# One upper-half copy of a weight tile moved between the two odd/even exponentials of the attention steps

## The chip, the cores and the metric

The kernel runs on one core of a Trainium2 chip. The metric is device time in microseconds (us) of one execution. The engines are named as in the profile: PE (TensorE, matmuls), PEld (its weight loads), DVE (VectorE), ACT (ScalarE), POOL (GpSimd) and SP (SyncE, which here only issues DMAs). Each engine carries out its own instructions in the order in which the program lists them, and engines wait for one another on semaphores.

## The reference, cut to what matters

A sequence of 256 tokens of width 1024 goes through a first block (a gated mixer, a neighbourhood attention and 64 experts) and then through a second block of two equal layers. The change touches only the attention part of these two layers:

```python
proj = x @ w_in            # q_sb k_sb v_sb q_mb k_mb v_mb g_sb g_mb
z = einsum(q_sb, k_sb) * scale                       # stick-breaking attention
log_keep = where(past, log_sigmoid(-z), 0)
suffix = cumsum(log_keep, reverse=True) - log_keep
w = where(past, exp(log_sigmoid(z) + suffix), 0)
o_sb = w @ v_sb
o_mb = moba_attention(rope(q_mb), rope(k_mb), v_mb)  # with 256 tokens a causal softmax attention
merged = sigmoid(g_sb) * (o_sb @ w_branch_sb) + sigmoid(g_mb) * (o_mb @ w_branch_moba)
x = layer_norm(alpha * x + merged @ w_out); x = layer_norm(alpha * x + swiglu(x))
```

## The kernel before

Large fp32 matmuls are made out of three passes over operands split in two: an upper half (the value rounded to fp32r) and a lower half (what is left). For every weight tile of 128 x 2048 values that lands in `weight_ring`, ACT writes the upper half (`high`, a Copy of the whole tile, line 1822) and DVE then subtracts it for the lower half (`low`, line 2494). PE waits for the lower half (`wait_split`) before it uses the tile. The upper halves have a few places (`high_place`), so `high` first waits until the weights have landed and until the job that last read its place is done (`wait_used`).

A layer's attention has six steps, p = 0 to 5: three of the stick-breaking attention (`p < NS`, NS = 3) and three of the other one. In each step PE runs, in this order: `scores(p)` (line 1438), `weighted_sum(p - 1)` (line 1464), the step's "fillers" (`FILLERS_OF_STEP`: parts of x @ w_in that do not depend on the attention, 24 matmuls of 512 columns each, line 957), and `weights_turn(p)` (eight transposes, line 908). Each filler output of 512 columns has two weight tiles, one for each half of the contraction, and two token tiles t = 0, 1. `NEXT_CHUNK[p]` names the two weight tiles of the next filler output, whose halves are made in step p: "vm" in step 0, "gs" 0 in step 1, "gs" 1 in step 2, then "gm" 0, "gm" 1 and "bs".

In a stick-breaking step the scores of the even heads (side 0) and of the odd heads (side 1) are in two banks. ACT takes the absolute value of both, Exp of both, Ln of both. DVE then makes the logarithm of the weights, first for side 0 and then for side 1 (`stick_b`, lines 2649 to 2663; each ends with an increment of `log_weights`). ACT takes Exp of side 0 and of side 1 as each is ready (line 1927), then makes the two upper halves of `NEXT_CHUNK[p]`, then moves out the remaining fillers (`gate_out`, line 1860), and then copies the transposed weights from their banks to `wT_` (`weights_out`, line 1870), for which the next step's `weighted_sum` waits. In step 2 ACT's order behind the filler of that step is thus: Exp side 0, Exp side 1, high, high, gate_out(7), weights_out(2). PE's order at that place is filler 7, weights_turn(2), scores(3), weighted_sum(2), filler 8.

The order of all this is written out by hand in the program. `NEXT_CHUNK`, the tiles' places in the rings and the semaphore counts follow from one list (`SPLIT_UNITS`), in whose order both ACT and DVE go through the tiles.

Of the kernel before, what the change touches and what calls it, by code (L numbers as in the profile page):

```python
# [156 lines left out]
NS = len(STEPS)  # L157
# [7 lines left out]
def plan():  # L165
# [188 lines left out]
    for r in (main, long, hold, units):  # L354
# [17 lines left out]
NEXT_CHUNK = {p: [("l_in", *name, half) for half in range(2)]  # L372
              for p, name in ((0, ("vm", 0)), (1, ("gs", 0)), (2, ("gs", 1)), (3, ("gm", 0)), (4, ("gm", 1)))}
# [24 lines left out]
def high_place(key, layer):  # L398

    if layer and key in FIRST_UNITS:  # L400
        return 4 + FIRST_UNITS.index(key)
    return HIGH_PLACE[SPLIT_UNITS.index(key)]
# [16 lines left out]
def build(nc, a):  # L419
    banks, units, freed_by, sources, order, last_jobs = plan()  # L420
    ctx = ExitStack()
    with ctx:
# [5 lines left out]
        def sem(name):  # L428
            if name not in sems:
                sems[name] = ctx.enter_context(nc.semaphore(name))  # L430
            return sems[name]
# [163 lines left out]
        def bank(key):  # L595
            return psum[banks[key][0]]
# [7 lines left out]
        def wait_full(eng, key, it=0):  # L604

            b, n, per = banks[key]
            eng.wait_ge(bank_full[b], n + 1 + it * per)
# [9 lines left out]
        def out(ins, key):  # L617
            ins.then_inc(bank_free[banks[key][0]], 1)
# [8 lines left out]
        def wait_weights(eng, key, it=0):  # L627
            s, n, per = units.place[key]
            eng.wait_ge(landed[s], 16 * (n + 1 + it * per))
# [11 lines left out]
        def upper(key, it):  # L641
            if key in FIRST_SPLIT:
                at = FIRST_UPPER[FIRST_SPLIT.index(key)]
                return ring_low[:, at, :] if at < SLOTS else first_upper[:, at - 10240:at - 10240 + SLOT]
            place = high_place(key, it)
            return high_ring[:, place, :] if place < 4 else high_late[:, (1, 2, 0)[place - 4], :]
# [7 lines left out]
        def wait_used(eng, key, it):  # L654
            job = freed_by[key]
            if job[0] == "down":
                eng.wait_ge(sem("down_done"), (FT // 2 - 1) * (it + 1) + job[1] + 1)
            else:
                wait_full(eng, job, it)
# [185 lines left out]
        def _(pool):  # L845
# [3 lines left out]
            for i, (col, n, _) in enumerate(pieces[:2]):  # L849
                pool.dma_start(bias[:, i, 0:n], bcast("b_in", col, n)).then_inc(sem(f"bias_landed{i}"), 16)  # L850
# [764 lines left out]
        def _(act):  # L1615
# [197 lines left out]
            def high(layer, *key):  # L1813

                u = SPLIT_UNITS.index(key)
                wait_weights(act, key, layer)
                earlier = [(l, v) for l in range(layer + 1) for v in range(NU) if (l, v) < (layer, u)]
                for l, v in reversed(earlier):
                    if high_place(SPLIT_UNITS[v], l) == high_place(key, layer):
                        wait_used(act, SPLIT_UNITS[v], l)  # L1820
                        break
                A(upper(key, layer), ring[:, units.place[key][0], :], ACT.Copy).then_inc(sem("high_ready"), 1)  # L1822
# [21 lines left out]
            for layer in range(L2):  # L1844
# [11 lines left out]
                def gate_out(i):  # L1856
                    name, n, t = FILLERS[i]
                    if name in ("gs", "gm"):
                        wait_full(act, (name, n, t), layer)
                        out(A(gates[("gs", "gm").index(name)][:, t, n * CHUNK:(n + 1) * CHUNK], bank((name, n, t))[:, :],  # L1860
                              ACT.Copy), (name, n, t))

                def sums_out(t):
                    wait_full(act, ("sums", t), layer)
                    out(A(inverse[0:2, :], bank(("sums", t))[0:2, :], ACT.Copy), ("sums", t))

                def weights_out(p):
                    for side in range(2):
                        wait_full(act, ("wT", p, side), layer)
                        out(A(wT_[:, side, :], bank(("wT", p, side))[:, :], ACT.Copy), ("wT", p, side))  # L1870

                def values_out(p):
                    b, t = p // NS, STEPS[p % NS][0]
                    if p % NS in LAST_OF_TILE:
                        act.wait_ge(sem("values_summed"), 2 * TT * layer + TT * b + t + 1)
                        values = bank(("o", b, t))[:, :].rearrange("p (f q) -> p f q", q=P)
                        if b == 0:
                            if t == 0:

                                wait_used(act, ("l_in", "km", 0, 0), layer)  # L1880
                            A(oTs[:, 0, :, t * P:(t + 1) * P], values, ACT.Copy).then_inc(sem("o_left_high"), 1)
                        else:
                            if t:
                                act.wait_ge(sem("o_right"), TT * layer + t)
                            out(A(o32, values, ACT.Copy), ("o", b, t))

                def values_high(t):
                    act.wait_ge(sem("o_scaled"), TT * layer + t + 1)
                    A(oTm[:, 0, :, t * P:(t + 1) * P], o32, ACT.Copy).then_inc(sem("o_right_high"), 1)

                for p in range(2 * NS):
                    t, fs = STEPS[p % NS]
                    keys = P * (t + 1)
                    if p < NS:
                        at = 2 * NS * layer + 2 * p
                        for side in range(2):
                            wait_full(act, ("sc", p, side), layer)
                            A(es[:, side, :], bank(("sc", p, side))[:, :], ACT.Abs).then_inc(sem("abs_ready"), 1)
                        for side in range(2):
                            act.wait_ge(sem("abs_ready"), at + side + 1)  # L1900
                            A(es[:, side, :], es[:, side, :], ACT.Exp, scale=-1.0).then_inc(sem("exp_done"), 1)
                        for side in range(2):
                            act.wait_ge(sem("exp_done"), at + side + 1)
                            A(es[:, side, :], es[:, side, :], ACT.Ln, bias=1.0).then_inc(sem("ln_done"), 1)
                    else:
                        for side in range(2):
                            act.wait_ge(sem("mb_max"), 2 * NS * layer + 2 * (p - NS) + side + 1)
                            for j, f in enumerate(fs):
                                hh = t * H2 + 2 * f + side
                                last = A(rw[:, side, j * keys:(j + 1) * keys], bank(("sc", p, side))[:, j * keys:(j + 1) * keys],  # L1910
                                         ACT.Exp, bias=mbn[:, hh:hh + 1], accum_out=mbs[:, hh:hh + 1])
                            out(last, ("sc", p, side))
                    if p:
                        values_out(p - 1)
                    gate_out(FILLERS_OF_STEP[p][0])
                    if p == NS - 1:
                        for name, dst in (("qmT", q2), ("kmT", k2)):
                            for t in range(TT):
                                wait_full(act, (name, t), layer)
                                A(dst[:, 0, :, t * P:(t + 1) * P], bank((name, t))[:, :].rearrange("p (f q) -> p f q", q=P),  # L1920
                                  ACT.Copy).then_inc(sem("heads_high"), 1)
                    if p == 2 * NS - 1:
                        values_high(0)
                    if p < NS:
                        for side in range(2):
                            act.wait_ge(sem("log_weights"), at + side + 1)
                            A(rw[:, side, :], rw[:, side, :], ACT.Exp).then_inc(sem("stick_weights"), 1)
                    if p == NS + 1:
                        sums_out(0)
                    if p in NEXT_CHUNK:  # L1930
                        for half in range(2):
                            high(layer, *NEXT_CHUNK[p][half])
                    for i in FILLERS_OF_STEP[p][1:]:
                        gate_out(i)
                    weights_out(p)
# [929 lines left out]
```

## Time and profile before

| | |
|---|---|
| median of 3 runs | 1672.85 us (1669.48 to 1673.49) |
| the profiled execution's own time | 1673.72 us |
| its span, first to last instruction | 1671.9 us |
| PE busy | 1612.7 us, 96% of the span |
| DVE / ACT busy | 842.9 us (50%) / 596.6 us (36%) |
| mean granted TensorE clock | 0.987 |
| attention steps of layer 0 / layer 1 in the trace | about 927 to 1036 us / 1316 to 1425 us |

The profile has a page of the whole span and views of the trace behind it: the waits of one engine, the instructions in order of time, and busy time with granted clock in given stretches. PE is busy nearly all the time, so a change on ACT can only matter where PE stands still or runs at its lower clock because of ACT. In a timeline row, "[2.65 <-ACT ...]" is the idle time of the engine just before this instruction and the engine that ended it. Durations of merged rows are from the first start to the last end; neighbouring rows of one engine can overlap a little, since instructions are pipelined.

### The profile page before, as it was taken

The page shows a single profiled execution, that of the slowest core. Times are in us where ns is not written, and L with a number is a line of the kernel's source. Part 1 is how long each engine was busy: PE and PEld are TensorE (multiplying, and loading weights), DVE is VectorE, ACT ScalarE, POOL GpSimd, SP SyncE. Part 2 cuts the span into 40 slices and gives each one's busy share as a digit, 9 for nine tenths or more (in the row PEclk, how much of TensorE's full clock was granted, in tenths as well). Part 3 has the DMA queues.
Part 4 walks back from the last instruction along what each step waited for, and adds up shares of the span by engine and source line. Part 5 has one row for each costly group of instructions (what it writes and reads, how often), then busy time and mean ns, then how long its engine had stood idle before and what let it go on. Part 6 is the DMA issues. An engine that isn't in the chain of part 4 may idle for free.

```text
span 1671.9 us, 21860 instructions
## 1 busy us (share of the span) xinstructions
PE 1612.7 (96%) x9158; PEld 1144.0 (68%) x9159; DVE 842.9 (50%) x1186; ACT 596.6 (36%) x815; POOL 27.7 (2%) x48
## 2 busy tenths in 40 slices
PE   5999999999999999999999999999999999999998
PEld 2975545874444444444447877799998877799997
DVE  3639825753222222222227765865447684865454
ACT  2504432321111111111124666444343565644432
POOL 0200010000000000000000000000000000000000
PEclk8999999999999999999999999999999999999999
DMA  9956874556999999999984435456445542555540
GB/s 357 235 198 239 308 274 176 196 201 258 421 421 421 420 421 421 421 421 421 421 323 145 153 116 198 144 187 213 166 153 200 177 150 103 201 178 200 165 163 25
DMA packets 148434, 418.55 MB, mean 250 GB/s; under 512 B 6977, under 2 KB 55249, under 8 KB 123313
## 3 DMA queue, kind: packets, MB, share of 16 engines
q1 hardware_dynamic: 126048, 271.19, 44.8%
q10 hardware_dynamic: 17568, 127.93, 18.4%
q0 software_dynamic: 4720, 18.03, 3.7%
q8 instruction: 74, 1.21, 0.3%
q14 instruction: 24, 0.19, 0.0%
HBM read 416.07 MB, written 2.95 MB: 251 GB/s over the span
## 4 chain that ended last, share of the span: by engine, by line
PE 90%; DVE 5%; ACT 2%; issue 1%; SPq 1%; DMA 1%; DVEq 0%; ACTq 0%
PE bank L957 20%; PE bank L1309 14%; PE bank L1603 12%; PE bank L1320 7%; PE bank L1553 6%; PE bank L1291 4%; PE bank L939 4%; PE bank L1330 4%; PE bank L972 3%; PE bank L908 3%; PE bank L1133 3%; PE bank L1574 3%; DVE ring_low L2494 1%; SPq L735 1%; DMA weight_ring<-in_w_ada 1%
## 5 line engine op out<-in xcount | busy, mean ns | idle before, releaser
L2494 DVE TENSOR_TENSOR ring_low<-weight_ring,high_ring 128x2048 fp32r<-128x2048 f32 x92 | 207.9, 2287 | 59.9 <-ACT high_ring L1822 59.5
L1309 PE MATMUL bank<-weight_ring,arena 128*64 128x512 f32 x800 | 232.1, 592 | 0.7 <-DVE arena L2414 0.7
L957 PE MATMUL bank<-high_ring,split 128*128 128x512 f32 x608 | 201.5, 406 | 0.2 <-DVE split L2501 0.2
L957 PE MATMUL bank<-ring_low,split 128*128 128x512 f32 x448 | 180.8, 404 | 0.0
L1309 PEld LDWEIGHTS bank<-weight_ring,arena 128*64 128x64 f32 x800 | 74.5, 137 | 150.2 <-issue 150.2
L1822 ACT ACTIVATE high_ring<-weight_ring 128x2048 fp32r<-128x2048 f32 x92 | 171.6, 1905 | 10.5 <-PE bank L957 5.9
L1603 PE MATMUL bank<-split,ring_low 128*128 128x256 f32 x576 | 162.6, 282 | 0.0
L1603 PE MATMUL bank<-split,high_ring 128*128 128x256 f32 x832 | 148.9, 281 | 0.0
L957 PEld LDWEIGHTS bank<-high_ring,split 128*128 128x128 f32 x608 | 117.7, 194 | 33.2 <-issue 3.4
L1603 PEld LDWEIGHTS bank<-split,high_ring 128*128 128x128 f32 x832 | 128.8, 189 | 0.7
L1320 PE MATMUL bank<-weight_ring,arena 128*64 128x512 f32 x400 | 120.5, 598 | 0.6 <-DVE arena L2414 0.6
L2473 DVE SCALAR_TENSOR_TENSOR arena<-bank,cols,arena 128x256 f32<-128x256 f32 x33 | 16.0, 484 | 193.0 <-ACT arena L1790 193.0
L1309 PE MATMUL bank<-arena 128*64 128x512 f32 x256 | 112.5, 592 | 0.0
L2488 DVE TENSOR_TENSOR split<-bank,split 128x512 fp32r<-128x512 f32 x66 | 45.6, 691 | 125.9 <-ACT split L1804 125.9
L1603 PEld LDWEIGHTS bank<-split,ring_low 128*128 128x128 f32 x576 | 108.8, 189 | 0.0
L957 PEld LDWEIGHTS bank<-ring_low,split 128*128 128x128 f32 x448 | 86.0, 192 | 17.8
L1804 ACT ACTIVATE split<-bank 128x512 fp32r<-128x512 f32 x66 | 39.4, 597 | 146.0 <-PE bank L1320 146.0
L1790 ACT ACTIVATE arena<-bank 128x256 f32<-128x256 f32 x33 | 12.7, 384 | 209.0 <-PE bank L1309 209.0
L1291 PEld LDWEIGHTS bank<-routed 128*128 128x128 f32 x544 | 66.7, 190 | 27.4 <-issue 27.4
L908 PE MATMUL bank<-const,arena 128*128 128x128 f32 (+1 forms) x530 | 75.9, 282 | 6.8 <-DVE arena L2755 3.0
L1320 PEld LDWEIGHTS bank<-weight_ring,arena 128*64 128x64 f32 x400 | 34.4, 136 | 68.6 <-issue 68.6
L2785 DVE TENSOR_TENSOR arena<-arena,bank 128x256 f32<-128x256 f32 x44 | 18.5, 420 | 122.0 <-ACT arena L1965 122.0
(327 smaller groups left out, 2796.5 us busy)
## 6 DMA issues: line engine op xcount, KB each, us to landing
weight_ring<-in_w_in SPq DMA_DIRECT2D x62, 1024.0 KB, 8.2
weight_ring<-in_w_e_gate SPq DMA_DIRECT2D x49, 1024.0 KB, 9.2
weight_ring<-in_w_e_up ACTq DMA_DIRECT2D x46, 1024.0 KB, 13.7
weight_ring<-in_w_e_down ACTq DMA_DIRECT2D x46, 1024.0 KB, 13.0
weight_ring<-in_w_ada SPq DMA_DIRECT2D x24, 1024.0 KB, 11.7
weight_ring<-in_w_ffn_gate SPq DMA_DIRECT2D x22, 1024.0 KB, 5.5
weight_ring<-in_w_ffn_up SPq DMA_DIRECT2D x22, 1024.0 KB, 8.1
weight_ring<-in_w_ffn_down SPq DMA_DIRECT2D x22, 1024.0 KB, 6.1
```

The costliest lines, as they stand in the source:

```text
L908: return nc.tensor.transpose(dst, src, k("ident")[0:m, 0:m])
L939: last = mm(bank(key)[:, 0:cols_], left[:, n, t * P:(t + 1) * P], wv[:, j, :], start=(n == 0), stop=(n == kts * len(units_) - 1))
L957: last = mm(bank(key)[:, :], left[a_][:, n, t * P:(t + 1) * P], wv[b_][:, j, :], start=(n == 0 and i == 0), stop=(n == kts * len(units_) - ...
L972: last = mm(bank(key)[:, s_ * S:(s_ + 1) * S], halves(uk, CHUNK, it)[a_][:, n % 4, f * P:(f + 1) * P], right[b_][:, n, :], start=(n == 0 a ...
L1291: last = mm(down_banks[j][:, s_ * QUAD * CAP:s_ * QUAD * CAP + n], h2s[:, part, t, kt, :], onehot[:, q % 2, t, 0:n], start=(t == 0 and par ...
L1309: last = mm(hidden_bank[side * CAP:(side + 1) * CAP, :].rearrange("p (j n) -> p j n", n=FF), xgT[:, p // 2 % 2, kt, at:at + CAP], hidden_u ...
L1320: last = mm(down_banks[n][side * CAP:(side + 1) * CAP, :], hidT[:, p % 2, at:at + CAP], down_unit(e % DOWN_UNITS)[:, f, n * CHUNK:(n + 1) ...
L1330: last = mm(y_bank(n, t)[:, :], sent[:, p % 3, t * P:(t + 1) * P], ys[:, part, n * CHUNK:(n + 1) * CHUNK], start=False, stop=(p == PAIRS a ...
L1553: last = mm(bank(key)[:, :], fh[:, (2 * d + f) % 4, a_, t * P:(t + 1) * P], wv[b_][:, f, n * CHUNK:(n + 1) * CHUNK], start=(d == 0 and f = ...
L1603: last = mm(bank(key)[:, j * S:(j + 1) * S], wv[a_][:, kt, f * P:(f + 1) * P], xs[:, b_, kt, :], start=(kt == 0 and i == 0), stop=(kt == K ...
L1822: A(upper(key, layer), ring[:, units.place[key][0], :], ACT.Copy).then_inc(sem("high_ready"), 1)
L2494: V.tensor_tensor(lower(key), ring[:, units.place[key][0], :], upper(key, layer), ALU.subtract)\
```

## The change

In steps 0, 1 and 2 of each layer the first of the two `high` copies of `NEXT_CHUNK[p]` is issued between Exp of side 0 and Exp of side 1; the second one stays where it was, behind Exp of side 1. Steps 3 to 5 keep both where they were. The order of the upper halves among themselves is the same, and nothing is added or left out. The diff:

```diff
@@ -1925,10 +1925,13 @@
                         for side in range(2):
                             act.wait_ge(sem("log_weights"), at + side + 1)
                             A(rw[:, side, :], rw[:, side, :], ACT.Exp).then_inc(sem("stick_weights"), 1)
+                            if side == 0:
+
+                                high(layer, *NEXT_CHUNK[p][0])
                     if p == NS + 1:
                         sums_out(0)
                     if p in NEXT_CHUNK:
-                        for half in range(2):
+                        for half in range(p < NS, 2):
                             high(layer, *NEXT_CHUNK[p][half])
                     for i in FILLERS_OF_STEP[p][1:]:
                         gate_out(i)
```

## Rows read from the trace of the kernel before

**Rows 1.** The page's chain of work that ended last, shares by engine.

```profile
PE 90%; DVE 5%; ACT 2%; issue 1%; SPq 1%; DMA 1%; DVEq 0%; ACTq 0%
```

**Rows 2.** PE's waits in 870 to 1130: us in total, times, longest us.

```profile
PE bank L1464 <- ACT arena L1870: 3.1, 2, 2.7
```

**Rows 3.** Timeline of ACT, layer 0, step 2: start us, us, instruction, [idle before].

```profile
980.00 0.63 ACT L1927 ACTIVATE arena<-arena 128x512 f32<-128x512 f32 x1
982.99 0.63 ACT L1927 ACTIVATE arena<-arena 128x512 f32<-128x512 f32 x1 [2.36 <-DVE arena L2663]
983.53 3.70 ACT L1822 ACTIVATE high_ring<-weight_ring 128x2048 fp32r<-128x2048 f32 x2
987.13 0.58 ACT L1860 ACTIVATE arena<-bank 128x512 f32<-128x512 f32 x1
987.61 1.07 ACT L1870 ACTIVATE arena<-bank 128x512 f32<-128x512 f32 x2
```

**Rows 4.** Timeline of PE, layer 0, ends of steps 0, 1 and 2.

```profile
948.96 1.09 PE L1464 MATMUL bank<-arena 128*64 128x128 f32 x16
...
966.77 1.03 PE L908 MATMUL bank<-const,arena 128*128 128x128 f32 x8
...
983.65 1.03 PE L908 MATMUL bank<-const,arena 128*128 128x128 f32 x8
...
988.83 1.09 PE L1464 MATMUL bank<-arena 128*64 128x128 f32 x16 [2.65 <-ACT arena L1870]
```

**Rows 5.** Timeline of DVE, layer 0, end of step 2.

```profile
982.53 0.42 DVE L2663 TENSOR_TENSOR arena<-arena,const 128x256 f32<-128x256 f32 x1
985.46 4.49 DVE L2494 TENSOR_TENSOR ring_low<-weight_ring,high_ring 128x2048 fp32r<-128x2048 f32 x2 [2.50 <-ACT high_ring L1822]
```

**Rows 6.** Timeline of PE, layer 1, the same place.

```profile
1377.34 1.98 PE L1464 MATMUL bank<-arena 128*64 128x128 f32 x16 [2.66 <-ACT arena L1870]
```

**Rows 7.** Stretches: us, busy PE PEld DVE ACT POOL, granted clock, DMA share, GB/s.

```profile
929.00:930.00 1.00, 1.00 (x4) 0.81 (x3) 1.00 (x1) 1.00 (x2) 0.00 (x0) 0.50 1.05 406
990.00:991.00 1.00, 1.00 (x4) 0.81 (x5) 0.97 (x2) 0.00 (x0) 0.00 (x0) 0.70 0.95 354
1376.00:1377.00 1.00, 0.00 (x0) 0.00 (x0) 1.00 (x2) 1.00 (x3) 0.00 (x0) 0.55 1.03 395
```

**Rows 8.** Timelines: weighted sum of step 3, and gate_out after the next filler tile.

```profile
997.27 0.60 ACT L1860 ACTIVATE arena<-bank 128x512 f32<-128x512 f32 x1 [2.23 <-PE bank L957]
...
1004.51 1.09 PE L1464 MATMUL bank<-arena 128*64 128x128 f32 x16
...
1011.39 0.60 ACT L1860 ACTIVATE arena<-bank 128x512 f32<-128x512 f32 x1 [2.62 <-PE bank L957]
...
1386.78 0.60 ACT L1860 ACTIVATE arena<-bank 128x512 f32<-128x512 f32 x1 [3.22 <-PE bank L957]
```

**Rows 9.** Timeline of PE, three other stops in layer 0.

```profile
927.14 1.56 PE L1438 MATMUL bank<-split 64*128 64x128 f32 x24 [1.67 <-issue]
...
977.39 0.66 PE L908 MATMUL bank<-const,arena 128*128 128x128 f32 x4 [0.56 <-DVE split L2710]
...
1061.87 1.10 PE L908 MATMUL bank<-const,arena 128*128 128x128 f32 x8 [1.51 <-DVE arena L2755]
```

**Rows 10.** Timeline of ACT, layer 0, steps 0 and 1.

```profile
943.60 0.63 ACT L1927 ACTIVATE arena<-arena 128x512 f32<-128x512 f32 x1 [3.55 <-DVE arena L2663]
...
950.02 1.15 ACT L1901 ACTIVATE arena<-arena 128x512 f32<-128x512 f32 x2
...
960.38 0.63 ACT L1927 ACTIVATE arena<-arena 128x512 f32<-128x512 f32 x1 [1.93 <-DVE arena L2663]
...
967.40 1.09 ACT L1870 ACTIVATE arena<-bank 128x512 f32<-128x512 f32 x2 [2.78 <-PE bank L908]
```

**Rows 11.** SP's load of gs 1, first tile; the page's median time to landing.

```profile
925.91 0.51 SPq L735 DMA_DIRECT2D weight_ring<-in_w_in  x1
...
weight_ring<-in_w_in SPq DMA_DIRECT2D x62, 1024.0 KB, 8.2
```

## Prediction

> **What bounds the kernel now.** I read the page's chain first: 90% of it is PE [rows 1]. ACT work that is moved is worth nothing unless PE stands still for it, so the next view is the list of PE's waits around the attention of layer 0. One line in it is ACT's to answer for: the weighted sum (line 1464) waited for `weights_out` (line 1870) twice, 3.1 us in all, of which one stop has 2.7 [rows 2]; layer 1 has the same line again with the same numbers. The timeline of PE puts the long one at the end of step 2: 2.65 us of idle time before 988.83 in layer 0 [rows 4] and 2.66 us before 1377.34 in layer 1 [rows 6]. The reader should see there that the stop begins at 988.83 - 2.65 = 986.18, where the scores of step 3 end, and that nothing but the two copies of line 1870 ends it.
>
> The timeline of ACT tells why these copies are late [rows 3]. Exp of side 0 ends at 980.63, ACT idles 2.36 us until DVE has the logarithms of side 1, and only then, in one unbroken row, come Exp side 1 (982.99), the two `high` copies (983.53 to 987.23), gate_out (987.13) and the two weights_out (987.61 to 988.68). PE starts 0.15 us later. From 982.99 on, ACT is the path and each microsecond of it is paid by PE, while 2.36 us of ACT just before were empty.
>
> A second cost hangs on the same stop: the clock. The granted clock is 0.70 in 990 to 991 and 0.55 in 1376 to 1377 [rows 7], which is a mixture of its two levels, 2.4 GHz (1.00) and 1.2 GHz (0.50). What a low clock does is read from equal work at either level. From the start of the weighted sum to the gate_out behind the first filler tile it is 1011.39 - 1004.51 = 6.88 us in step 4, at full clock, but 997.27 - 988.83 = 8.44 us behind the stop in layer 0 and 1386.78 - 1377.34 = 9.44 us in layer 1 [rows 4, 6, 8]. So the clock costs 1.56 us in layer 0 and 2.56 us in layer 1, 4.12 us together.
>
> **The change, part by part.**
>
> *Step 2, where PE waits.* A pair of `high` copies lasts 3.70 us, and from the first start to the gate_out behind them it is 987.13 - 983.53 = 3.60 us, so one copy takes 1.80 us of ACT's sequence and about 1.90 us from start to end [rows 3]. Placed behind Exp side 0 (which lets its successor begin some 0.1 us before its end, at 980.54 as 983.53 follows 982.99) it runs to 982.44. DVE's last operation for side 1 ends at 982.53 + 0.42 = 982.95 [rows 5], so Exp side 1 still starts at 982.99, with 0.5 us to spare. Behind it now stands one copy and not two: gate_out comes at 985.33, weights_out at 985.81 to 986.88, and PE's weighted sum 0.15 us later, at 987.03. The stop shrinks from 2.65 to 0.85 us. That is 1.80 us per layer, 3.60 us for both; layer 1 has the same intervals [rows 6]. gate_out itself does not become the later one: its filler ends where the transposes begin, at 983.65 [rows 4].
>
> *What could hold the moved copy.* It waits for its weights, for its place, and for nothing else. The first tile of gs 1 is issued by SP at 925.91, and the median load of this kind lands in 8.2 us, so near 934 [rows 11]. Its place was last read by the fillers of vm, which end where the transposes of step 1 start, at 966.77 [rows 4]. Both are more than 13 us before 980.5. SP itself waits for PE's banks, not for `high`, so no load moves because of the copy; POOL has no part in this.
>
> *Activation tables.* The copy now stands between two Exps. In step 0 the same Copy already runs behind the Exps, and the next Exp, at 950.02, follows copies and absolute values with no table load ahead of it [rows 10]. I count zero. Were there a reload after every copy, it would show as rows of their own; the trace has none.
>
> *DVE.* Its order is unchanged. The lower halves of gs 1 begin today at 985.46, 2.50 us of them idle time spent on ACT [rows 5]. With the upper half ready at 982.44, the first can begin at 982.95; the second waits for the second copy, which still starts at 983.53 and now ends at 985.43, and takes about 2.25 us, half of the pair's 4.49. So DVE is done near 987.7 and not at 989.95. PE's next filler, at 987.03 + 1.02 = 988.05, finds both, and DVE's share of step 3 begins 2.2 us sooner, more than PE's 1.80. What is next late for the weighted sum is still ACT (0.85 us: the second copy), not DVE.
>
> *Steps 0 and 1: costed at nothing.* ACT idles 3.55 us (step 0) and 1.93 us (step 1) before Exp side 1 [rows 10], so the copy of 1.80 to 1.90 us fits in both, in step 1 with hardly anything over. But nobody waits for what follows. In step 0 the weighted sum at 948.96 has no idle time before it [rows 4], and in step 1 weights_out waits 2.78 us for PE's transposes [rows 10]. The cover is PE's filler; if it were gone, step 1 would lose the 0.0 to 0.1 us by which the copy may outlast ACT's gap, and it would gain, not lose, up to the 1.80 us. Bounds for both steps: 0.1 us lost to 0.1 us gained for each layer; I take 0.
>
> *The clock.* The trace does not show a stop of 0.85 us at this place, so its cost is bounded from both sides: 0 (the clock stays up, all 4.12 us come back) to 4.12 us (it falls as now). The nearest rows: a stop of 0.56 us at 977.39 left the clock at 1.00, and even 1.51 us before 1061.87 did, with dense work around it; 1.67 us before 927.14, followed by short matmuls, brought it to 0.50 [rows 7, 9]. In layer 1 the clock fell when PE had been idle from 1374.68 to somewhat past 1376 (0.55 over 1376 to 1377), that is after over 1.3 us of idle time [rows 6, 7]. In layer 0 the first 0.8 us of the stop, with the same transposes and scores ahead of it, passed without a fall; the drop came in 990 to 991, after all 2.65 us. 0.85 is nearest to 0.56 and below each stop that cost anything, so I take 0 and keep the other end for the range.
> The Trainium skill, "TensorE: Matmul & The Clock Gate", section "What's actually happening", says that the low clock is the default, that activity releases it, and that the moment of judgement does not start with the kernel, so that runs of one kernel differ. The trace agrees: the same stop of 2.65 us brought the fall after its end in layer 0 and within it in layer 1. By that page a short stop can still fall in a bad moment, which is the second rival below.
>
> *Sum.* 3.60 us of shorter stops + 4.12 us of clock = 7.72 us. Against the profiled execution: 1673.72 - 7.7 = 1666.0. That execution lies 0.87 us above the median of 1672.85, against which the same gain gives 1665.1. I put the time at 1665.6, between them. Later work follows PE: the loads are released by PE's banks, and later stops, such as that of 1.51 us at 1061.87, are made of a chain that itself starts from PE's results, so I expect the whole gain to reach the end.
>
> **The rivals.**
>
> *A. Forecast: both stops shrink and the clock holds.* 1665.6 us, own range 1663 to 1667.5 (the runs before spread over 4 us). Chance 0.63.
>
> *B. The stops shrink but the clock falls all the same.* The stretch of transposes, short score matmuls, 0.85 us of idle time and the short weighted sum is still thin work. Both layers lose the clock: 1672.85 - 3.6 = 1669.2, or 1670.1 from the profiled execution; in one layer only, about 1667.6. For it: 1.67 us at 927.14 was enough there. Against: that is twice as long. Chance 0.13 for both layers, 0.12 for one.
>
> *C. The move gives nothing at the end.* Something behind step 2 takes the gain back: for example DVE's maxima of step 3 or the fillers' weights. It would be 1672 to 1673. Against it: no row of PE's waits between 988.83 and the end of step 3, and DVE gains more than PE. Chance 0.07. That the change does not do what it says would look the same; I see no way to it, as ACT's order is the program's.
>
> *D. Slower: the moved copy is held and blocks Exp side 1.* ACT runs in order, so Exp side 1, the transposes behind it (PE at 983.65) and weights_out queue behind the copy. If it starts X later than 980.54, Exp side 1 starts at 982.44 + X. The saving of 1.80 us and the spare 0.55 us are used up at X = 2.35, so from a release at 982.9 on the kernel is slower, by 2 us for every further microsecond (two layers); more than 5 us slower needs a release behind 985.4, giving 1678 or more. Against: load and place are ready near 934 and at 966.77. The remaining mishap is low-clock stretches at new places, some 1.6 to 2.6 us each. Chance 0.05.
>
> **How the numbers follow.** 0.3% of the time, 5.0 us, is about what a measurement of this kernel can tell from no change, so "faster" means below 1667.8. A counts as faster nearly whole (0.61 of 0.63), as does most of the one-layer case (0.08 of 0.12). B in both layers, C and the rest are within 0.3%: 0.26 with part of D. Slower: 0.03. Hence faster 0.70, same 0.27, slower 0.03. The range leaves out C and D at the top and ends with B at 1670.3; at the low end it allows for the spread of the runs, one of which lay 3.4 us below the median: 1662.5.
>
> **What the profile of the changed kernel would show.** In step 2 of each layer, a single `high` between the two Exps of line 1927, Exp side 1 still 2.99 us behind Exp side 0, and one `high` behind it; the wait of line 1464 for line 1870 at 0.8 to 0.9 us in place of 2.65; a granted clock of 1.00 over the filler that follows. If the stop is 0.85 and the clock 0.5 behind it, B is right. If Exp side 1 starts late, D is. If line 1464 starts 1.8 us earlier and some later wait is that much longer, C is. The prediction is wrong in its larger half (4.12 of 7.72 us) if the clock does not follow the stop's length.

## The result and the profile after

| | kernel before | changed kernel |
|---|---|---|
| median of 6 runs each, side by side on one chip | 1670.04 us (1667.20 to 1673.49) | 1662.22 us (1660.95 to 1664.54) |
| ratio, 95% interval | | 0.9948 (0.9938 to 0.9958) |
| profiled execution / its span | 1673.72 / 1671.9 us | 1662.30 / 1660.5 us |
| mean granted clock | 0.987 | 0.992 |

The kernel is faster by 0.52%: 0.0052 x 1670 = 8.7 us (7.0 to 10.4). The two medians themselves differ by 7.8 us, which lies in the same interval. The forecast was 7.7 us less than before and 1665.6 us, with a range from 1662.5 to 1670.3. The direction and the size of the gain came out; the time itself lies 0.28 us below the range.

The timeline of ACT, layer 0, end of step 2, of the changed kernel answers to [rows 3]: start us, us, instruction, [idle before].

```profile
976.03 0.63 ACT L1927 ACTIVATE arena<-arena 128x512 f32<-128x512 f32 x1
976.57 1.90 ACT L1822 ACTIVATE high_ring<-weight_ring 128x2048 fp32r<-128x2048 f32 x1
979.03 0.63 ACT L1927 ACTIVATE arena<-arena 128x512 f32<-128x512 f32 x1 [0.56 <-DVE arena L2666]
979.57 1.90 ACT L1822 ACTIVATE high_ring<-weight_ring 128x2048 fp32r<-128x2048 f32 x1
981.37 0.58 ACT L1860 ACTIVATE arena<-bank 128x512 f32<-128x512 f32 x1
981.84 1.07 ACT L1870 ACTIVATE arena<-bank 128x512 f32<-128x512 f32 x2
```

Exp side 1 starts 979.03 - 976.03 = 3.00 us behind Exp side 0, against 2.99 in [rows 3]: the moved copy delays nothing, with 0.56 us to spare. There is no table load between the copy and the Exp. The trace does have rows of table loads (ACT_TABLE_LOAD, 1.28 us each), one ahead of each pair of Lns and one ahead of Exp side 0, in both kernels; where the prediction says that the trace has none, it holds only for the places behind a copy that stands between Exps. From Exp side 1 to the first weights_out it is 2.81 us and was 4.62. The timelines of PE (layer 0 and layer 1) and of DVE answer to [rows 4, 6, 5]:

```profile
983.06 1.09 PE L1464 MATMUL bank<-arena 128*64 128x128 f32 x16 [0.82 <-ACT arena L1870]
...
1368.28 1.09 PE L1464 MATMUL bank<-arena 128*64 128x128 f32 x16 [0.83 <-ACT arena L1870]
```

```profile
978.57 0.42 DVE L2666 TENSOR_TENSOR arena<-arena,const 128x256 f32<-128x256 f32 x1
978.91 2.28 DVE L2497 TENSOR_TENSOR ring_low<-weight_ring,high_ring 128x2048 fp32r<-128x2048 f32 x1
981.50 2.29 DVE L2497 TENSOR_TENSOR ring_low<-weight_ring,high_ring 128x2048 fp32r<-128x2048 f32 x1 [0.30 <-ACT high_ring L1822]
```

The stop has shrunk from 2.65 to 0.82 us, and DVE makes the first lower half without waiting, as worked out. The stretches behind the stops, to be read with [rows 7] (us, busy PE PEld DVE ACT POOL, granted clock, DMA share, GB/s):

```profile
984.00:991.00 7.00, 7.00 (x34) 5.62 (x31) 3.41 (x7) 4.54 (x19) 0.00 (x0) 1.00 0.45 171
1369.00:1376.00 7.00, 7.00 (x37) 5.59 (x33) 3.63 (x8) 4.34 (x19) 0.00 (x0) 1.00 0.47 178
```

The clock is at its upper level, 2.4 GHz, in both layers. In layer 0, from the weighted sum to the next gate_out it is now 989.97 - 983.06 = 6.91 us, where it was 8.44:

```profile
989.97 0.60 ACT L1860 ACTIVATE arena<-bank 128x512 f32<-128x512 f32 x1 [1.08 <-PE bank L957]
```

The profiled spans differ by 11.4 us, which is more than the change did. Three steps of the chain in order of time divide it, first of the kernel before, then of the changed one: the keys' matmuls ahead of the attention of layer 0, and the first long group of the feed-forward part in each layer.

```profile
902.75 22.72 PE bank L972 x192
1092.71 14.39 PE bank L1574 x120
1482.11 14.39 PE bank L1574 x120
```

```profile
898.79 22.72 PE bank L972 x192
1085.51 14.39 PE bank L1574 x120
1470.67 14.39 PE bank L1574 x120
```

Up to the first the changed kernel is 3.96 us ahead, before anything of the change has run. From the first to the second it gains 189.96 - 186.72 = 3.24 us, from the second to the third 389.40 - 385.16 = 4.24 us, and behind that nothing (0.04 us). So the change itself is worth 7.5 us in this pair of profiles, and the other 4 us belong to the two executions. In the fourteen profiles at hand the keys' matmuls of layer 0 start between 898.79 and 902.75 us, and not by kernel: s2_only, which has the move in step 2 as well, starts them at 902.61. The kernel before has the latest start of all. The 4 us arise in the first 43 us, where PE waits for the first loads and the clock is low for some time (over 35 to 40 us it is 0.50 before and 0.76 after); in the chain or the timeline of PE it is this row, before and after:

```profile
42.64 13.43 PE bank L939 x64
```

```profile
38.75 13.41 PE bank L939 x64
```

### The profile page after: what moved, and what is told of

Its sections match the earlier page's. It is cut to its first block, busy times and chain, and to the rows that moved or that the text cites. A ratio compares the mean times of both kernels' runs of the same rounds, so it can differ in the third digit from the quotient of the medians.

```text
span 1660.5 us, 21860 instructions
## 1 busy us (share of the span) xinstructions
PE 1606.6 (97%) x9158; PEld 1139.0 (69%) x9159; DVE 842.8 (51%) x1186; ACT 597.2 (36%) x815; POOL 27.6 (2%) x48
## 4 chain that ended last, share of the span: by engine, by line
PE 90%; DVE 5%; ACT 1%; issue 1%; SPq 1%; DMA 1%; DVEq 0%
PE bank L957 20%; PE bank L1309 14%; PE bank L1603 12%; PE bank L1320 7%; PE bank L1553 6%; PE bank L1291 4%; PE bank L939 4%; PE bank L1330 4%; PE bank L972 3%; PE bank L908 3%; PE bank L1133 3%; PE bank L1574 3%; DVE ring_low L2497 1%; SPq L735 1%; DMA weight_ring<-in_w_ada 1%
## 5 line engine op out<-in xcount | busy, mean ns | idle before, releaser
L1822 ACT ACTIVATE high_ring<-weight_ring 128x2048 fp32r<-128x2048 f32 x92 | 172.3, 1906 | 10.4 <-PE bank L957 5.8
```

## The experiments

The runs were made in three groups, each compared with the kernel before on the same chip: 1671.92 us (median of 15 runs) for s2_only, s01_only, both_between and early; 1671.30 (21 runs) for fill_stop2, fill_stop0_before, fill_stop0_after and fill_stop0_early; 1670.81 (23 runs) for fill_stop2_short, fill_stop0_short_before, fill_stop0_short_early and pad512. A line behind an inserted one has a higher number in that run's rows: the weighted sum, 1464, can be L1465 or L1466, and weights_out, 1870, can be L1871 to L1873. Stops are in us, of the one profiled execution of each.

| run | ratio, 95% interval | stop of the weighted sum, end of step 0 (layer 0, 1) | end of step 2 | low clock behind step 2's stop |
|---|---|---|---|---|
| kernel before | 1 | 0, 0 | 2.65, 2.66 | both layers |
| changed kernel | 0.9948 (0.9938 to 0.9958) | 0, 0 | 0.82, 0.83 | none |
| s2_only | 0.9955 (0.9941 to 0.9969) | 0, 1.46 | 0.86, 0.86 | none |
| s01_only | 0.9986 (0.9976 to 0.9997) | 0, 0 | 2.67, 2.63 | layer 0 |
| both_between | 0.9942 (0.9929 to 0.9956) | 0, 0 | 0, 0 (0.56 at the transposes) | none |
| early | 0.9936 (0.9922 to 0.9949) | 0, 0 | 0, 0 | none |
| fill_stop2 | 1.0000 (0.9991 to 1.0009) | 0, 1.56 | filled, too long | none |
| fill_stop2_short | 0.9985 (0.9977 to 0.9994) | 0, 1.60 | filled, 0.70 and 0.71 left | none |
| fill_stop0_before | 1.0005 (0.9995 to 1.0014) | 0.62, 0.72 | 2.63, 2.66 | both |
| fill_stop0_after | 0.9945 (0.9932 to 0.9959) | 0, 0 | 0.86, 0.83 | none |
| fill_stop0_early | 0.9940 (0.9926 to 0.9953) | 0, 0 | 0, 0 | none |
| fill_stop0_short_before | 0.9994 (0.9985 to 1.0002) | 1.60, 1.59 | 2.66, 2.62 | both |
| fill_stop0_short_early | 0.9933 (0.9920 to 0.9946) | 0, 0 | 0, 0 | none |
| pad512 | 0.9961 (0.9948 to 0.9974) | 0, 0 | 1.49, 1.53 | layer 0 |

### Which step brings the gain

The move in step 2 alone (against the changed kernel):

```diff
-                            if side == 0:
+                            if side == 0 and p == NS - 1:
...
-                        for half in range(p < NS, 2):
+                        for half in range(p == NS - 1, 2):
```

> The copy is moved between the two Exps in step 2 alone; steps 0 and 1 are as before. Theory 1 (everything comes from step 2): the whole gain, 7.7 to 8.7 us, ratio to the kernel before 0.9948 to 0.9954; line 1464's stop 0.82 us in both layers, granted clock 1.00 behind it. Theory 2 (steps 0 and 1 bring part of it): ratio 0.9965 or more, while the stop is 0.82 us all the same.

Measured: 0.9955, and 0.86 us in both layers, with the clock at 1.00 behind it. Theory 1 holds in the main. But the profile has a row that nothing in the forecast allowed for, a new stop at the end of step 0 of layer 1 (timeline of PE), and the stretch of step 0 just before it:

```profile
1333.80 1.09 PE L1464 MATMUL bank<-arena 128*64 128x128 f32 x16 [1.46 <-ACT arena L1870]
```

```profile
1312.00:1318.00 6.00, 5.99 (x43) 5.11 (x44) 4.50 (x2) 5.97 (x7) 0.00 (x0) 1.00 0.92 339
```

The clock, which the kernel before lost in step 0 in both layers of its profile, was 1.00 here. PE came to the end of step 0 earlier and found ACT late. This became theory 3: in step 0, where the copy is not moved, the low clock had hidden the same ordering of ACT. The trace of the kernel before bears it out. There, in layer 0, ACT's copies of line 1870 at the end of step 0 are these (timeline of ACT):

```profile
947.75 1.06 ACT L1870 ACTIVATE arena<-bank 128x512 f32<-128x512 f32 x2
```

They end at 948.81, and the weighted sum starts 0.15 us later, at 948.96 [rows 4], the same interval as behind the stop of step 2. PE, slowed by its clock, and ACT arrived together. That the row showed no idle time did not mean that there was time to spare.

The move in steps 0 and 1 alone, the complement (`p < NS - 1` in both places):

> The copy is moved in steps 0 and 1 alone. Theory 1: ratio 1.000 (0.999 to 1.001); line 1464's stop at the end of step 2 stays at 2.65 us with low clock in its wake. Theory 2: 0.9985 or less. The copy in step 1 outlasts ACT's gap by at most 0.1 us, which nobody waits for.

Measured: 0.9986, its interval just short of 1. The stops at the end of step 2 are as in the kernel before, as expected, but layer 1 kept its clock this time. The timeline of PE and the stretch behind it:

```profile
1375.06 1.09 PE L1464 MATMUL bank<-arena 128*64 128x128 f32 x16 [2.63 <-ACT arena L1870]
```

```profile
1372.00:1380.00 8.00, 5.37 (x41) 4.38 (x40) 7.12 (x8) 5.13 (x17) 0.00 (x0) 1.00 0.68 258
```

So neither theory had it right: steps 0 and 1 seem to bring a little (2.3 us by the ratio, 0.5 to 4.0), but the profiled execution, with low clock in step 0 of both layers, shows no place where they did. From the start of the keys' matmuls to the first long group of the feed-forward part, layer 0 takes 190.85 us (189.96 in the kernel before) and layer 1 188.17 (190.75). Both differences are, to within 0.1 us, the clock behind the stop of step 2, which cost 0.95 us more in layer 0 and 2.53 us less in layer 1.

### What queues behind the moved copy

Both copies of step 2 between the two Exps, which makes Exp side 1 wait:

```diff
                             if side == 0:

                                 high(layer, *NEXT_CHUNK[p][0])
+                                if p == NS - 1:
+                                    high(layer, *NEXT_CHUNK[p][1])
```

> In step 2 both copies stand between the two Exps (steps 0 and 1 as in the changed kernel). It tests that ACT's order makes Exp of side 1 wait: both copies together last 3.70 us against a gap of 2.4, so Exp side 1 should start 1.2 us late, and PE's odd transposes 0.6 us late. If the path is ACT's sum of work from there, as I hold, weights_out comes 0.5 us sooner than in the changed kernel while PE arrives 0.6 us later: the stop of line 1464 falls to about 0 and the time is that of the changed kernel within 0.5 us (ratio 0.994 to 0.996). The rival (holding Exp side 1 back is costly by itself): 2 us per layer slower than the changed kernel, ratio 0.997 or more.

Measured: 0.9942. The rows are of ACT and of PE, layer 0:

```profile
977.80 0.63 ACT L1927 ACTIVATE arena<-arena 128x512 f32<-128x512 f32 x1
978.34 3.71 ACT L1822 ACTIVATE high_ring<-weight_ring 128x2048 fp32r<-128x2048 f32 x2
981.95 0.61 ACT L1927 ACTIVATE arena<-arena 128x512 f32<-128x512 f32 x1
```

```profile
982.61 0.66 PE L908 MATMUL bank<-const,arena 128*128 128x128 f32 x4 [0.56 <-ACT arena L1927]
...
984.69 1.09 PE L1464 MATMUL bank<-arena 128*64 128x128 f32 x16
```

Exp side 1 starts 4.15 us behind Exp side 0 and no longer 3.00; PE stops 0.56 us in its transposes and not at all at the weighted sum. Holding the Exp back by 1.15 us moved the stop and cost nothing more. That bears out how rival D was priced (a short hold is free), and that nothing in the changed kernel came near its point of decision.

### Removing the stop that was left

```diff
+                    if p == NS - 1:
+                        high(layer, *NEXT_CHUNK[p][0])
                     gate_out(FILLERS_OF_STEP[p][0])
...
-                                high(layer, *NEXT_CHUNK[p][0])
+                                high(layer, *NEXT_CHUNK[p][p == NS - 1])
...
-                        for half in range(p < NS, 2):
+                        for half in range(2 if p == NS - 1 else p < NS, 2):
```

> In step 2 the first copy goes ahead of gate_out(6), into ACT's idle time of 2.19 us behind the Lns, and the second one between the two Exps; steps 0 and 1 as in the changed kernel. Theory: the remaining stop of 0.82 us in each layer goes too, since nothing but gate_out stands between Exp side 1 and weights_out: 1.6 us less than the changed kernel, ratio to the kernel before 0.9938 to 0.9945. Rival: DVE becomes the late one (lower halves of gs 1 or the maxima of step 3) or the transposes' own latency remains, and the ratio is that of the changed kernel.

Measured: 0.9936, 1660.74 us. The first copy fits the gap, ACT reaches weights_out while the second half of the transposes is still running, and PE does not stop (timelines of ACT and PE, layer 0):

```profile
969.57 1.90 ACT L1822 ACTIVATE high_ring<-weight_ring 128x2048 fp32r<-128x2048 f32 x1
971.84 0.60 ACT L1860 ACTIVATE arena<-bank 128x512 f32<-128x512 f32 x1 [0.37 <-PE bank L957]
```

```profile
982.44 1.09 PE L1464 MATMUL bank<-arena 128*64 128x128 f32 x16
```

The ratio is 0.0002 below the range expected and 1.2 thousandths (2 us) below the changed kernel's, though the two intervals overlap. With the run of fill_stop0_short_early below it is the fastest measured here. In this profile the clock fell in step 0 in layer 0 only.

### The clock's part by itself

The kernel before with matmuls of constants in the stop of step 2, so that only the clock can change:

```diff
                     scores(p)
+                    if p == NS:
+                        keep_busy(("gs", 1, 0), 5, layer)
```

> The kernel before with five matmuls of constants (512 columns, about 0.43 us apart, results unused) for PE between the scores of step 3 and the weighted sum, in the stop of 2.65 us; ACT's order is untouched, so the weighted sum still starts when line 1870 is done. It takes the clock's part alone. Theory (the clock falls because PE stands still there): granted clock 1.00 behind the stop in both layers and no change in the stop's end; up to 4.1 us faster, less where the kernel before did not lose the clock in a run: ratio 0.9975 to 0.999. Rival (the clock falls from thin work before and after, whatever is in the stop, or the matmuls are in the way): clock 0.50 there as before, ratio 1.000 or more.

Measured: 1.0000. The pacing was wrong: five took 4.56 us, and the weighted sum started 1.8 us later than ACT would have allowed (the row with x10 is the five, two instructions each).

```profile
983.87 4.56 PE L983 MATMUL bank<-const 128*128 128x512 f32 x10
988.36 1.09 PE L1464 MATMUL bank<-arena 128*64 128x128 f32 x16
```

Twice 1.8 us lost and no gain or loss in all means that about as much came back through the clock, but two unknowns stand against each other there. With 2 in place of 5:

> The run with matmuls of constants in the stop of 2.65 us, made again with two of them: they proved to take 0.91 us each, so that five (4.56 us) pushed the weighted sum 1.8 us back. Two take 1.8 us and leave 0.8 us idle; line 1464 should start where line 1870 ends, as in the kernel before. Theory: clock 1.00 behind the stop in both layers, 2 to 4 us faster, ratio 0.9976 to 0.9988 (the kernel before loses the clock there in five of six looks). Rival: ratio 1.000.

Measured: 0.9985 (0.9977 to 0.9994), that is 2.5 us (1.0 to 3.8), with the rest of the stop still ended by line 1870 and the clock at 1.00 behind it in both layers:

```profile
986.92 1.09 PE L1464 MATMUL bank<-arena 128*64 128x128 f32 x16 [0.70 <-ACT arena L1872]
...
1373.72 1.09 PE L1464 MATMUL bank<-arena 128*64 128x128 f32 x16 [0.71 <-ACT arena L1872]
```

```profile
986.00:993.00 7.00, 6.30 (x39) 5.02 (x39) 4.98 (x7) 4.13 (x19) 0.00 (x0) 1.00 0.46 177
```

The clock's part exists apart from the stop's length, and PE's standing still there brings it about: with most of the stop filled, the same thin work on either side of it ran at 1.00. As a mean over runs it is smaller than the 4.1 us of the one profile, which lies just outside the interval.

### Step 0 with its cover taken away

The same kind of matmuls in PE's stop of 1.67 us ahead of step 0 [rows 9], so that the clock holds through step 0, in the kernel before and in the changed one:

```diff
+                keep_busy(("sc", 0, 0), 3, layer)
                 for name in ("qs", "ks", "vs"):
                     for p in range(2):
                         wait_out(pe, (name, p), layer)
```

> The kernel before with three such matmuls in PE's stop of 1.67 us ahead of step 0's scores, so that the clock holds through step 0's fillers. Theory 3 (new, from the run with step 2 alone: where the clock happened to hold in step 0, the weighted sum of step 0 waited 1.46 us for ACT): the low clock of step 0 hides the late Exp and copies there. Then PE comes 1.6 us sooner to the end of step 0 and waits about 1.5 us for line 1870, in both layers: gain near nothing, ratio 0.999 to 1.000. If step 0 costs nothing as I had predicted: no such stop, 3.2 us faster, ratio 0.998.

> The changed kernel with the same three matmuls. Theory 3: the copy moved in step 0 now counts, no stop of line 1464 at the end of step 0, so the 1.6 us of clock come through in both layers: 3.2 us less than the changed kernel, ratio to the kernel before near 0.993; against the kernel before with the same matmuls the move is then worth 10 to 11 us. If theory 3 is wrong, the two kernels with the matmuls differ by the same 8.7 us as the two without.

Measured: 1.0005 and 0.9945. The three took 2.74 us, 1.07 more than the stop, so that most of the clock's 1.6 us was spent again, and neither kernel became faster. What can be read is the end of step 0 (timeline of PE), first without the move, then with it:

```profile
947.12 1.09 PE L1465 MATMUL bank<-arena 128*64 128x128 f32 x16 [0.62 <-ACT arena L1871]
```

```profile
948.16 1.09 PE L1465 MATMUL bank<-arena 128*64 128x128 f32 x16
```

The pair differs by 0.9945 / 1.0005 = 0.9940, 10 us, where the pair without them differs by 8.7: in the sense of theory 3, but within the intervals. The stops, 0.62 and 0.72 us against none, are the firmer evidence. With 1.35 us of matmuls (one of 512 columns and one of 256), in the kernel before:

```diff
+                keep_busy(("sc", 0, 0), 1, layer)
+                mm(bank(("sc", 0, 0))[:, 0:S], k("ident"), const[:, 0:S], start=True, stop=True)
```

> The kernel before with 1.35 us of such matmuls in the stop of 1.67 us ahead of step 0 (2.74 us proved too long: it pushed the scores back by 1.07 us). Theory 3: clock 1.00 in step 0, and line 1464 stops for about 1.5 us at the end of step 0 in both layers, so the 1.6 us of clock are lost again: ratio 0.9995 to 1.0005. If step 0 costs nothing: no stop, ratio 0.998.

Measured: 0.9994 (0.9985 to 1.0002), beside the 0.9995 to 1.0005 of theory 3 and clear of 0.998, with the clock held and the stop there in both layers:

```profile
947.02 1.09 PE L1466 MATMUL bank<-arena 128*64 128x128 f32 x16 [1.60 <-ACT arena L1872]
...
1335.42 1.10 PE L1466 MATMUL bank<-arena 128*64 128x128 f32 x16 [1.59 <-ACT arena L1872]
```

```profile
927.00:935.00 8.00, 8.00 (x36) 6.47 (x36) 5.25 (x5) 7.92 (x10) 0.00 (x0) 1.00 0.49 187
```

A step 0 with full clock gives its 1.6 us straight to a stop for ACT unless the copy is moved. Both versions of the matmuls were also put into the kernel called early:

> The run called early (first copy of step 2 in ACT's idle time behind the Lns, second one between the Exps) together with the three matmuls in the stop ahead of step 0. If the gains add up: 1.6 us from the stop at the end of step 2 and 3.2 us from step 0's clock, ratio to the kernel before 0.991 to 0.992, the fastest of all.

> The same short matmuls with the run called early. Theory 3: no stop of line 1464 in steps 0 and 2, clock 1.00 in both; 3.2 us less than early alone where early loses the clock in step 0: ratio 0.9915 to 0.993. If early alone is as fast, the clock of step 0 is not to be had this way.

Measured: 0.9940 and 0.9933, against 0.9936 of early alone. The clock was 1.00 in step 0 and the weighted sum did not stop, in both, but the 3.2 us did not come. Both profiles lost their clock instead between the layers, where that of early alone kept it: it was 0.57 over 1275 to 1279 with the three and 0.57 over 1277 to 1281 with the short ones. The medians (1660.10 and 1660.74 us, different chips) cannot tell what reached the end. The traces can tell what arrived inside a layer. The chain in order of time has the starts of the keys' matmuls and of the first long group of the feed-forward part, in layers 0 and 1, first for s2_only, then for early:

```profile
902.61 22.72 PE bank L972 x192
1089.05 14.39 PE bank L1574 x120
1287.62 22.73 PE bank L972 x192
1474.22 14.39 PE bank L1574 x120
```

```profile
899.23 22.72 PE bank L972 x192
1084.77 14.39 PE bank L1574 x120
1283.34 22.72 PE bank L972 x192
1467.54 14.39 PE bank L1574 x120
```

Each of these two executions lost the clock of step 0 in layer 0 and kept it in layer 1. With the copy of step 0 where it was (s2_only), the layers take 186.44 and 186.60 us: the clock kept brings nothing. With the copy moved (early) they take 185.54 and 184.20 us: it brings 1.34 us. In fill_stop0_short_early, with the clock kept in both, they take 184.02 and 183.83. Where the state of the clock is the same, two layers of one execution differ by 0.2 us. So step 0's clock is worth 1.3 to 1.5 us per layer once the copy is moved, and nothing before. Part of the 3.2 us expected was never there to gain, since early keeps the clock of layer 1 in some of its executions anyway.

### Part of the stop put back

The changed kernel with one more Copy of 512 columns ahead of the second upper half of gs 1:

```diff
+                if key == ("l_in", "gs", 1, 1):
+                    A(upper(key, layer)[:, 0:512], ring[:, units.place[key][0], 0:512], ACT.Copy).then_inc(sem("pad"), 1)
+                    act.wait_ge(sem("pad"), layer + 1)
```

> The changed kernel with one more Copy of 512 columns, and a wait for it, ahead of the second upper half in step 2: the stop of line 1464 should grow from 0.82 to about 1.5 us. The stop alone costs 2 x 0.65 = 1.3 us: ratio 0.9955 to 0.996. If the clock falls at stops of this length, as it did behind 1.67 us of idle time ahead of step 0, 1.6 us or more per layer come on top: ratio 0.997 to 0.998.

Measured: 0.9961 (0.9948 to 0.9974), between the two ranges expected and unable to tell them apart. The profile shows both outcomes: stops of 1.49 and 1.53 us, and in layer 0 the weighted sum takes 1.98 us at low clock, in layer 1 it takes 1.09.

```profile
984.54 1.98 PE L1464 MATMUL bank<-arena 128*64 128x128 f32 x16 [1.49 <-ACT arena L1873]
...
1371.78 1.09 PE L1464 MATMUL bank<-arena 128*64 128x128 f32 x16 [1.53 <-ACT arena L1873]
```

## Why the prediction was right or wrong, point by point

- **The path through ACT, step 2: right.** The stop was to shrink from 2.65 to 0.85 us and measured 0.82 and 0.83. The bounds on what could hold the copy, the zero for table loads and the order of DVE's lower halves held too. s2_only has nearly the whole gain, 0.9955 against 0.9948.
- **The clock, 4.12 us: right in kind, too large as a mean.** It stayed at 1.00 behind all six stops of 0.82 to 0.86 us that were profiled (changed kernel, s2_only, fill_stop0_after). But the 2.65 us stop does not always cost it, nor always the same: it did in seven of eight cases (kernel before, s01_only, fill_stop0_before, fill_stop0_short_before, two layers each). From the weighted sum to the gate_out these took 8.44 and 9.44, 9.39 and 6.91, 8.42 and 8.44, 8.46 and 9.46 us, against 6.88 at full clock, which is 3.5 us per execution on the mean. (The rows that the prediction names for the stops at 977.39 and 1061.87 do not show the clock there; the trace has 1.00 at both.) The fill run, which takes the clock's part alone, gives 2.5 us (1.0 to 3.8). The step of the forecast that failed here is that one profile's 1.56 and 2.56 us were taken for every execution's.
- **Steps 0 and 1 at nothing: wrong for step 0.** The forecast named PE's filler as the cover and said what its loss would be worth (up to 1.80 us), but did not see that this filler ran long only because its clock was low. In nine kernels with the stop ahead of step 0 left alone (both kernels, s2_only, s01_only, both_between, early, the two runs that fill step 2's stop, pad512), the clock held in 5 of 18 cases, in layer 1 each time. Where it holds and the copy is not moved, the stop is 1.5 to 1.6 us; where it holds and the copy is moved, the layer is 1.3 to 1.5 us shorter (s2_only and early above). An estimate from these counts: 5/18 x 2 layers x 1.55 us = 0.9 us per execution. The 0.9986 of s01_only (2.3 us, 0.5 to 4.0) is compatible with that size and does not prove it. Step 1 shows no stop in any profile, and its copy just fits ACT's gap. In the changed kernel Exp side 1 starts 2.55 us behind Exp side 0 (timeline of ACT, layer 0, step 1), where it was 2.56 in the kernel before, with no idle time left before it that the profile shows:

```profile
953.79 0.63 ACT L1927 ACTIVATE arena<-arena 128x512 f32<-128x512 f32 x1
954.32 1.91 ACT L1822 ACTIVATE high_ring<-weight_ring 128x2048 fp32r<-128x2048 f32 x1
956.34 0.63 ACT L1927 ACTIVATE arena<-arena 128x512 f32<-128x512 f32 x1
```

- **The sum: right, by terms that err both ways.** 3.60 (measured 3.66) + 2.5 to 3.5 for the clock + some 0.9 for step 0 = 7.1 to 8.1 us (an estimate), beside 8.7 (7.0 to 10.4) by the ratio. The forecast's 7.7 lies in both.
- **The time and the range: wrong, through the base.** This is the step that put the measured time outside the range: the gain was taken off 1673.72 us (the profiled execution) and 1672.85 (the median of three runs). Those three runs were high: with three more the median of the kernel before is 1670.04, and on the other chips 1670.81 to 1671.92. 7.7 us off 1670.04 is 1662.3, the measured time. The forecast knew a spread of 4 us in the runs and used it for the low end of the range, not for the base of the sum.
- **The rivals.** B (the clock falls at the short stop) was not seen once in six cases at 0.8 us; at 1.5 us in the same place it came once in two. C did not occur: in the two profiles step 2 itself gives 2 x 1.83 us of stop and 1.53 + 2.53 us of clock, 7.7 us, and 7.5 of them reach the end. D did not occur, and both_between shows that even a hold of 1.15 us is absorbed.

## What to carry to other kernels

When an engine's row of work is on the path and it idles just ahead of that row, move into the gap whatever has its operands and whose reader is not the next in line; count the gap, the piece and the spare (here 2.36, 1.80 and 0.56 us), and look for the stop at its far end. A zero for "covered by the other engine" is only as good as that engine's speed in the profile at hand: see whether the cover ran at low clock, and cost the case in which it does not. And set a sum against as many runs of the kernel before as there are; three runs spread over 4 us moved the base by 2.8 us, a third of the effect.

## What the runs showed of the hardware that had not been expected

The same idle time can keep or lose TensorE's clock from one layer to the next in one execution: 1.67 us ahead of step 0 lost it in all nine cases in layer 0 and in four of nine in layer 1; 1.5 us at the end of step 2 lost it once and kept it once; 1.46 to 1.60 us at the end of step 0 kept it in all five cases (s2_only, fill_stop2 and fill_stop2_short in layer 1, fill_stop0_short_before in both); 2.6 us kept it once in eight. When it was lost, it stayed at 0.50 for some 3 to 7 us, and the weighted sum of 1.09 us took up to 1.98. Filling the idle time with matmuls whose results nobody uses kept it at 1.00 behind the filled stop in all 14 cases (seven runs, two layers). Their price was a surprise too: 0.91 us for one fp32 matmul of 512 columns, against 0.23 us from one to the next in the three-pass fillers. The kernel before shows it already, where it runs 14 such instructions in 6.17 us (line 983, at 877.68), two instructions to a matmul.

The Trainium skill, "TensorE: Matmul & The Clock Gate", section "What's actually happening", says that the low clock is the default, released by activity, and judged at moments that do not follow the kernel's start. These counts agree with that, and no run here shows the moments themselves.
